# Two-layer hybrid block: the output projection's products reordered, and its first weights split within the scan

## The chip, the cores and the metric

The kernel runs on one core of one Trainium2 chip. A core has a matrix engine (TensorE, PE in the profile; PEld is its weight load), VectorE (DVE), ScalarE (ACT), GpSimd (POOL), a queue engine (SyncE, SP), an on-chip memory and a small accumulator memory (psum) that PE writes to. The metric is the device time of one execution in microseconds, lower is better.

## What is computed

Two layers of a block over 512 latent tokens and 256 context tokens, width 1024, in float32. The first layer's mixer is a bidirectional state-space scan beside a long convolution with a filter made by a small network; the second's is windowed attention. Both are followed by a gated feed-forward. The part that the change touches:

```python
def finish(y, z, hy):
    b, L = z.shape[:2]
    y = rmsnorm(y.reshape(b, L, SSD_WIDTH) * jax.nn.silu(z.astype(jnp.float32)), norm_g).astype(z.dtype)
    g = hyena_op(hy, hy_conv_w, hy_conv_b, hy_filt, hy_bias)
    return jnp.concatenate([y, g], axis=-1) @ w_out
...
        x = x + mod_l[2] * o_l
```

Here `y` is the scan's result, `g` the long convolution's ("Hyena"), and `w_out` the output projection, 2048 rows to 1024 columns.

## The kernel before

The activations lie feature by token: `X` (residual), `HN` (normed), eight tiles of 128 features by 768 tokens. Every product of this precision is made of three: a float32 value is split into a high part (a copy rounded to the fast format) and a low part (value minus high part), and PE adds high weight x high input, low weight x high input, and high weight x low input. A tile's three products run over 512 and 256 columns (`SEGS`).

Weights come in jobs (`JOBS`) of two halves, eight tiles of 128x128 each, into three slots in turn (`W[:, s]`). SyncE loads a half once the products that used its slot are counted in `blocks_done`. VectorE makes the high half (`split_high`, line 1623) into `WH`, of which there is one for both halves of a job; GpSimd makes the low half in the slot itself (`low`, line 2146, tile `weights_lo`). Each engine runs its own program in order and waits on counting semaphores; the order is written by hand.

The accumulators are three pairs of banks, `pair(0)` to `pair(2)`; a pair is free again when its reader has counted up `pair_free`.

The stages that matter, in order of time:
- The filter stage ends with twelve spectral products of the filter (`kd_mm`), each followed by a copy of one bank on ScalarE (line 1255) and two sums on VectorE (lines 1668 to 1672, counted in `kd_ev`). Meanwhile the first norm is applied: VectorE scales a tile of `X` into `HN` (`tile_first`, line 1616), ScalarE adds the shift (line 1215) and copies the high part (line 1217, `high_parts`), GpSimd makes the low part (line 2160). PE waits for all twelve `kd_ev` and starts the first input projection, `uv`, tile by tile (`both_by_tile`, lines 539 to 545).
- The scan: twelve steps, written as turns of two (`chunk_turns`). In a step PE makes the heads' products (943) in four groups, the score masks (904, 908), the spread decay (918), the carried product (928) and the states (951). ScalarE takes exponentials (1409, 1422); VectorE weighs the scores (`weigh`, 1873), multiplies the carried part (1880), adds it (1887) and adds the states (1894); GpSimd adds the carried part (`add_carried`, 2237), scales the input (2245) and the states (2253) and decays to the end (2262). Parts of two weight slots and the memory from 27648 on in `R` hold operands of the scan, and the last of these overlaps `WH`.
- The output projection, `out0` and `out0b`. Its first three jobs, G0 to G0+2, hold six half blocks: the Hyena parts of output tiles 0, 1 and 2, then the gated (scan) parts of the same three, so that PE can begin with Hyena inputs (`YGH[:, 1]`, `YGL[1]`, tile `hyena_lo`) while the scan's result is gated (VectorE, line 1926), squared and summed (ACT 1446, DVE 1932), normed through PE (`token_sums` 620, `token_spread` 626), scaled (DVE 1942) and split (ACT 1451, POOL 2291, tile `ssd_lo`). ScalarE's splits of both kinds are counted in `mix_hi`, GpSimd's in `mix_lo`. In the code before, G0 is cast when the scan is over, its two halves run tile by tile with highs and lows in turn, and the other four half blocks run one after another. VectorE adds each finished output tile to `X` (`residual`, 1959) and sums its squares (1599, 1600).

## Time and profile before

| | before |
|---|---|
| median of 3 runs | 2230.56 us (2226.12 to 2230.6) |
| the profiled execution's own time | 2231.3 us |
| its span | 2229.5 us |
| mean granted clock of PE | 0.967 of full |
| PE busy | 2111.7 us, 95% |
| weight load, DVE, ACT, POOL busy | 1682.1, 860.5, 441.2, 811.3 us |
| PE's share of the chain that ended last | 87% |

The span is the profiled part of one execution. Busy times are sums over the whole of it, and PE's are modelled, since its matmuls are pipelined. The granted clock has two levels, 1.2 GHz (0.50) and 2.4 GHz (1.00).

### The profile page before, as it was taken

To read this page: it belongs to the slowest core of one execution; us is meant where nothing else is said; L and a number is where in the kernel's file an instruction comes from. 1 tells how busy PE (TensorE), PEld (TensorE's weight loads), DVE (VectorE), ACT (ScalarE), POOL (GpSimd) and SP (SyncE) were. 2 spreads that over 40 slices of the span, in tenths; PEclk is the share of its full clock that TensorE was granted. 3 is DMA by queue.
4 is the path that set the end of the run, shared out by engine and by line. 5 is a ranking of instruction groups with operands and counts; after the bars stand their busy time and mean duration, and the time that the engine had idled before them with its cause. 6 is when DMAs were issued, how large, how long until landed. Compare 5 with 4: busy or idle time off the path is not lost.

```text
span 2229.5 us, 29888 instructions
## 1 busy us (share of the span) xinstructions
PE 2111.7 (95%) x11842; PEld 1682.1 (75%) x11842; DVE 860.5 (39%) x1245; ACT 441.2 (20%) x830; POOL 811.3 (36%) x438
## 2 busy tenths in 40 slices
PE   7989999999989978999999999998889999999997
PEld 2477668877877767878888888887666677888886
DVE  4633545203337664332121122233346663322334
ACT  3331110012335541031010010102026602100110
POOL 1443537122227755243223232224310134444443
PEclk9999989999989989999999999998989999999999
DMA  9444324342110011212112211121210022223222
GB/s 386 158 137 143 120 89 135 113 146 100 48 57 1 1 46 50 66 48 66 56 49 66 76 67 62 43 65 57 96 38 1 1 76 76 88 84 111 94 74 77
DMA packets 50791, 182.31 MB, mean 82 GB/s; under 512 B 5568, under 2 KB 6080, under 8 KB 49664
## 3 DMA queue, kind: packets, MB, share of 16 engines
q1 hardware_dynamic: 49600, 171.92, 22.8%
q10 hardware_dynamic: 576, 5.97, 0.7%
q0 software_dynamic: 512, 2.95, 0.4%
q8 instruction: 76, 1.25, 0.2%
q14 instruction: 27, 0.22, 0.0%
HBM read 178.72 MB, written 2.10 MB: 81 GB/s over the span
## 4 chain that ended last, share of the span: by engine, by line
PE 87%; DVE 5%; POOL 3%; ACT 2%; DMA 2%; issue 1%; DVEq 0%; ACTq 0%; SPq 0%
PE psum L516 21%; PE psum L521 21%; PE psum L517 21%; PE psum L1102 2%; PE psum L1090 2%; PE psum L1119 2%; PE psum L583 1%; PE psum L703 1%; DMA weights<-in_wall 1%; PE psum L739 1%; PE psum L918 1%; PE psum L539 1%; PE psum L545 1%; PE psum L943 1%; PE psum L540 1%
## 5 line engine op out<-in xcount | busy, mean ns | idle before, releaser
L2146 POOL TENSOR_TENSOR weights_lo<-weights,weights_hi 128x1024 fp32r<-128x1024 f32 (+1 forms) x228 | 504.9, 2215 | 989.4 <-DVE weights_hi L1623 989.4
L1623 DVE CAST weights_hi<-weights 128x1024 fp32r<-128x1024 f32 (+1 forms) x232 | 166.7, 720 | 887.1 <-PE psum L521 741.4
L521 PE MATMUL psum<-normed_lo,weights_hi 128*128 128x512 f32 x1760 | 506.9, 351 | 0.0
L516 PE MATMUL psum<-normed_hi,weights_hi 128*128 128x512 f32 x1088 | 391.6, 360 | 6.7 <-DVE weights_lo L1719 3.8
L517 PE MATMUL psum<-normed_hi,weights_lo 128*128 128x512 f32 x1088 | 373.9, 358 | 0.0
L521 PEld LDWEIGHTS psum<-normed_lo,weights_hi 128*128 128x128 f32 x1760 | 284.3, 189 | 16.5
L516 PEld LDWEIGHTS psum<-normed_hi,weights_hi 128*128 128x128 f32 x1088 | 204.8, 188 | 56.7 <-POOL weights_lo L2146 4.3
L516 PE MATMUL psum<-normed_first_hi,weights_hi 128*128 128x512 f32 (+1 forms) x672 | 232.2, 346 | 2.5 <-DVE weights_lo L1719 2.0
L517 PEld LDWEIGHTS psum<-normed_hi,weights_lo 128*128 128x128 f32 x1088 | 205.5, 189 | 34.8 <-issue 1.0
L517 PE MATMUL psum<-normed_first_hi,weights_lo 128*128 128x512 f32 (+1 forms) x672 | 212.7, 338 | 0.0
L516 PE MATMUL psum<-hidden_hi,weights_hi 128*128 128x512 f32 (+1 forms) x528 | 189.1, 358 | 0.0
L517 PE MATMUL psum<-hidden_hi,weights_lo 128*128 128x512 f32 (+1 forms) x528 | 178.9, 354 | 0.0
L521 PE MATMUL psum<-hidden_lo,weights_hi 128*128 128x512 f32 (+1 forms) x528 | 160.4, 358 | 0.0
L516 PEld LDWEIGHTS psum<-normed_first_hi,weights_hi 128*128 128x128 f32 x672 | 127.2, 189 | 38.2 <-issue 7.6
L517 PEld LDWEIGHTS psum<-normed_first_hi,weights_lo 128*128 128x128 f32 x672 | 127.2, 189 | 16.3 <-issue 1.2
L516 PEld LDWEIGHTS psum<-hidden_hi,weights_hi 128*128 128x128 f32 x528 | 99.1, 188 | 23.4
L517 PEld LDWEIGHTS psum<-hidden_hi,weights_lo 128*128 128x128 f32 x528 | 99.4, 188 | 15.1
L1731 DVE SCALAR_TENSOR_TENSOR temps<-psum,vectors,temps 128x511 f32<-128x511 f32 x112 | 63.8, 612 | 99.2 <-ACT temps L1277 98.3
L1468 ACT ACTIVATE temps<-psum 128x768 f32<-128x768 f32 (+1 forms) x44 | 31.1, 708 | 358.3 <-PE psum L521 353.8
L1472 ACT ACTIVATE hidden_hi<-temps 128x768 f32 (+3 forms) x44 | 32.6, 740 | 332.1 <-DVE temps L2013 332.1
L521 PEld LDWEIGHTS psum<-hidden_lo,weights_hi 128*128 128x128 f32 x528 | 87.1, 188 | 8.9
L516 PE MATMUL psum<-mixed_hi,weights_hi 128*128 128x512 f32 x224 | 77.8, 347 | 8.5 <-POOL weights_lo L2146 8.5
(312 smaller groups left out, 2973.1 us busy)
## 6 DMA issues: line engine op xcount, KB each, us to landing
weights<-in_wall SPq DMA_DIRECT2D x264, 512.0 KB, 3.9
weights<-in_wall SPq DMA_DIRECT2D x32, 384.0 KB, 3.2
weights<-in_wall SPq DMA_DIRECT2D x32, 320.0 KB, 3.0
residual<-in_xT SPq DMA_DIRECT2D x1, 3072.0 KB, 16.9
residual<-in_xT ACTq DMA_DIRECT2D x1, 3072.0 KB, 11.1
phase<-in_tab ACTq DMA_DIRECT2D x2, 1280.0 KB, 5.5
normed<-in_window SPq DMA_DIRECT2D x1, 1536.0 KB, 12.6
normed<-in_window POOLq DMA_DIRECT2D x1, 1536.0 KB, 9.5
```

The source lines that it names most:

```text
L516: mm(acc[:, lo:hi], WH[:, b, k, :], high[:, lo:hi], start=st, stop=False)
L517: mm(acc[:, lo:hi], WL[:, s, HALF * b + k, :], high[:, lo:hi], start=False, stop=False)
L521: ins = mm(acc[:, lo:hi], WH[:, b, k, :], low[:, lo:hi], start=False, stop=en)
L539: mm(accs[b][:, lo:hi], WH[:, b, k, :], high[:, lo:hi], start=k == 0, stop=False)
L1090: ins = mm(PSF[:, 1024 * e + at0:1024 * e + at1], QT[rows, 2 * g + j, b * P:b * P + P], KD[rows, g, key:key + at1 - at0], start=c in (0, 2 ...
L1102: ins = pe.transpose(PSF[:, 2048 + t * P:2048 + t * P + P], EX[:, n % 4, 1 + t * P:1 + t * P + P], C[:, IDENT, :])
L1119: ins = mm(PS[64 * e:64 * e + 64, 6, 0:256].rearrange("p (j c) -> p j c", j=2), VT[:, kt, 64 * g:64 * g + 64], heads_e, start=t == 0, stop ...
L1468: run(T[:, 0, lo:hi], pair(0)[:, lo:hi], ACT.Silu).then_inc(pair_free[0], 1)
L1472: run(at_row(HIDH, r)[:, lo:hi], T[:, 1, lo:hi], ACT.Copy).then_inc(hid_hi, 1)
L1623: dve.tensor_copy(WH[:, b, 0:n, :], W[:, s, HALF * b:HALF * b + n, :]).then_inc(w_hi, 1)
L1731: ins = STT(t[:, a:e], p[:, a + shift:e + shift], w, t[:, a:e], ALU.mult, ALU.add)
L2146: TT(WL[:, s, at, :], W[:, s, at, :], WH[:, b, 0:width(gs[0], b), :].bitcast(f32), ALU.subtract).then_inc(w_lo, 1)
```

## The change

At the end of the filter stage, ScalarE shifts only tile 0 between the last two bank copies (`shifted`) and splits it after the last one; VectorE scales tiles 0 and 1 as before but all others after the last pair of sums. At the projection, G0's halves are cast on VectorE and made low on GpSimd between the scan's first turns (`between`), into a home of their own, `WHX`, that lies where tiles 5 to 7 of `X` will be; G0+2 uses that home too, so that G0+1's is not waited for. PE runs all eight high products of G0's two halves first, then the lows, filling in the third half block's highs; the gated half blocks run all highs, then the lows of all three tile by tile. `X` is loaded in two parts, tiles 0 to 4 by ScalarE's queue as before and 5 to 7 by SyncE's after the six half blocks.

```diff
+        WHX = part("weights_first_hi", x_at, 4096, 2, HALF, P)
+        high_home = lambda g: WHX if g in (G0, G0 + 2) else WH
...
             body(0, (None, 4, 5, 5), False)
+            if between:
+                between(0)
             body(2, (5, 5, 4, 0), False)
+            if between:
+                between(1)
...
+                if at == G0 + 6:
+                    sp.wait_ge(blocks_done, 2 * G0 + 6)
+                    sp.dma_start(X[:, 5:KT, :], A["xT"][:, 5:KT, :]).then_inc(x2_in, 16)
...
-            both_by_tile([G0], 0, mixed, SEGS, mixed_waits, between_tiles, False)
...
+            def high_products(g, b, u, k, start):
+
+                s = g % SLOTS
+                high, _ = mixed(k)
+                for lo, hi in SEGS:
+                    mm(pair(u)[:, lo:hi], high_home(g)[:, b, k % KT, :], high[:, lo:hi], start=start, stop=False)
+                    mm(pair(u)[:, lo:hi], WL[:, s, HALF * b + k % KT, :], high[:, lo:hi], start=False, stop=False)
...
+            for b in range(2):
+                half_ready([G0], 0, b)
+                pair_ready([G0], 0, b)
+            for k in range(KT):
+                mixed_waits[0](k)
+                for b in range(2):
+                    high_products(G0, b, b, k, k == 0)
+            for k in range(KT):
+                mixed_waits[1](k)
+                for b in range(2):
+                    low_products(G0, b, b, k, False)
+                if k == 3:
+                    pe.wait_ge(yz_added, KT)
                     pe.wait_ge(yz_sums, 1)
                     token_sums(6).then_inc(yz_summed, 1)
-                if k == 7 and blocks == (0,):
+                    half_ready([G0 + 1], 0, 0)
+                    pair_ready([G0 + 1], 0, 0)
+                if k == 4:
                     pe.wait_ge(yz_rec, 1)
                     token_spread(6).then_inc(yz_spread, 1)
...
+                for h in ((), (), (), (0, 1), (2, 3), (4, 5), (6,), (7,))[k]:
+                    high_products(G0 + 1, 0, 2, h, h == 0)
+            for k in range(KT):
+                low_products(G0 + 1, 0, 2, k, False)
+
+            gated_parts = ((G0 + 1, 1, 0), (G0 + 2, 0, 1), (G0 + 2, 1, 2))
+            for g, b, u in gated_parts:
                 half_ready([g], 0, b)
-                tiles([g], pair(u), b, KT, gated, SEGS, False, True, gated_waits if u == 0 else None)
+                for k in range(KT):
+                    if u == 0:
+                        mixed_waits[0](KT + k)
+                    high_products(g, b, u, KT + k, False)
+            for k in range(KT):
+                mixed_waits[1](KT + k)
+                for g, b, u in gated_parts:
+                    low_products(g, b, u, KT + k, k == KT - 1)
...
-                    if n >= 10:
-                        high_parts(0, 0, 0, high=HNH0, ks=range(2) if n == 10 else range(2, KT))
+                    if n == 10:
+                        shifted(0, 0, 0, 0)
+            high_parts(0, 0, 0, high=HNH0, done=1)
...
-            act.dma_start(X[:, :, :], A["xT"]).then_inc(x_in, 16)
+            act.dma_start(X[:, 0:5, :], A["xT"][:, 0:5, :]).then_inc(x_in, 16)
...
-                        for k in (range(2), range(2, 4), range(4, KT))[n - 9]:
+                        for k in (range(2), (), range(2, KT))[n - 9]:
...
-            chunk_turns(dve, turn)
+            chunk_turns(dve, turn, between=lambda b: split_high([G0], 0, b))
...
-            for b in range(2):
-                split_high([G0], 0, b)
             for k in range(KT):
+                if k == 5:
+                    split_high([G0 + 1], 0, 0)
                 TT(XBC[:, k, :], XBC[:, k, :], Z[:, k, :], ALU.mult).then_inc(yz_ready, 1)
...
+                    dve.wait_ge(blocks_done, 2 * G0 + 3)
+                    split_high([G0 + 3], 0, 0)
                     for k in range(3):
+                        dve.wait_ge(blocks_done, 2 * G0 + 4 + k)
+                        if k == 0:
+                            split_high([G0 + 3], 0, 1)
                         residual(X[:, k, :], k, k)
...
-            chunk_turns(pool, turn)
-
-            low([G0], 0)
+            chunk_turns(pool, turn, between=lambda b: low([G0], 0, (b,)))
+            low([G0 + 1], 0, (0,))
```

The order on ScalarE at the end of the filter stage, from the eleventh bank copy on: `psum` to `phase` is the bank copy, `normed` with `mods` the shift, `normed_first_hi` the high part. Before:

```order
L1255 ACTIVATE phase<-psum 128x512 [waits kd_mm] x2
L1215 ACTIVATE normed<-normed,mods 128x512 [waits norm_mul]
L1215 ACTIVATE normed<-normed,mods 128x256
L1217 ACTIVATE normed_first_hi_53<-normed 128x768 [waits act_order]
L1215 ACTIVATE normed<-normed,mods 128x512 [waits norm_mul]
L1215 ACTIVATE normed<-normed,mods 128x256
L1217 ACTIVATE normed_first_hi_53<-normed 128x768 [waits act_order]
L1255 ACTIVATE phase<-psum 128x512 [waits kd_mm]
```

And with the change:

```order
L1304 ACTIVATE phase<-psum 128x512 [waits kd_mm] x2
L1258 ACTIVATE normed<-normed,mods 128x512 [waits norm_mul]
L1258 ACTIVATE normed<-normed,mods 128x256
L1304 ACTIVATE phase<-psum 128x512 [waits kd_mm,act_order]
L1266 ACTIVATE normed_first_hi_54<-normed 128x768
L1258 ACTIVATE normed<-normed,mods 128x512 [waits norm_mul]
```

The twelfth bank copy stands behind one shift instead of behind two whole tiles. On VectorE, the end of the scan and what follows (`phase<-phase` 128x768 is the gating multiply, `temps<-temps,psum` the sum of squares, the scaling reads `vectors` and `psum`). Before:

```order
L1887 TENSOR_TENSOR phase<-phase,psum 128x4x128 [waits step_y,step_zadd]
L1623 CAST weights_hi_49<-weights 128x1024 [waits w_loaded10,step_b,step_added]
L1623 CAST weights_hi_49<-weights 128x1024 [waits w_loaded11]
L1926 TENSOR_TENSOR phase<-phase 128x768 x8
L1934 COPY temps<-psum 128x768 [waits yz_square]
L1932 TENSOR_TENSOR temps<-temps,psum 128x768 [waits yz_added,yz_square] x7
L1937 MEMSET mark 128x1 [waits yz_added]
L1939 RECIPROCAL temps<-temps 128x12 [waits norm_sqrt]
L1942 SCALAR_TENSOR_TENSOR phase<-phase,vectors,psum 128x768 [waits yz_spread]
```

And with the change:

```order
L1937 TENSOR_TENSOR phase<-phase,psum 128x4x128 [waits step_y,step_zadd]
L1976 TENSOR_TENSOR phase<-phase 128x768 [waits step_b,step_added]
L1976 TENSOR_TENSOR phase<-phase 128x768 x4
L1673 CAST weights_hi_49<-weights 128x1024 [waits w_loaded20]
L1976 TENSOR_TENSOR phase<-phase 128x768 x3
L1984 COPY temps<-psum 128x768 [waits yz_square]
L1982 TENSOR_TENSOR temps<-temps,psum 128x768 [waits yz_added,yz_square] x7
L1987 MEMSET mark 128x1 [waits yz_added]
L1673 CAST weights_hi_49<-weights 128x1024 [waits w_loaded21]
```

The two casts of G0 are gone from here, and the first cast of G0+1 stands between the fifth and the sixth multiply. On GpSimd, one of the two places in the scan where a low part of G0 now stands, with the change (`phase<-phase,normed` adds the carried part, the three after it scale the input, the states and the decay to the end; before, the same rows stand without the second one):

```order
L2293 TENSOR_TENSOR phase<-phase,normed 128x4x128 [waits step_ze] x2
L2202 TENSOR_TENSOR weights_lo_50<-weights,weights_first_hi_51 128x1024 [waits weights_hi_ready]
L2301 TENSOR_TENSOR weights<-phase,temps 128x1024 [waits step_xde,step_y]
L2309 TENSOR_TENSOR temps<-temps 128x1024 [waits step_z]
L2318 TENSOR_TENSOR normed<-normed,temps 128x1024 [waits step_st,step_xdt]
```

What was done after the scan stands between the carried part and the next input's scaling.

## Rows read from the trace of the kernel before

**Rows 1.** PE's waits from 780 to 910 us: total, times, longest.
```profile
PE psum L516 <- POOL weights_lo L2146: 8.5, 1, 8.5
PE psum L539 <- POOL weights_lo L2146: 7.6, 1, 7.6
PE psum L545 <- POOL hyena_lo L2291: 4.9, 1, 4.9
```

**Rows 2.** Timeline of PE: start, duration, line, tiles, count [idle before].
```profile
800.52 0.66 PE L943 MATMUL psum<-normed,weights 128*64 128x128 f32 x8 [1.17 <-DVE normed L1873]
...
821.27 0.40 PE L539 MATMUL psum<-mixed_hi,weights_hi 128*128 128x512 f32 x1
...
822.67 0.86 PE L545 MATMUL psum<-hyena_lo,weights_hi 128*128 128x512 f32 x4
823.36 0.39 PE L539 MATMUL psum<-mixed_hi,weights_hi 128*128 128x512 f32 x1
...
829.69 1.39 PE L620 MATMUL psum<-consts,temps 128*128 128x2 f32 x12
...
833.13 1.50 PE L626 MATMUL psum<-consts,temps 128*128 128x128 f32 x12
```

**Rows 3.** Timeline of DVE in the projection's first part.
```profile
802.02 1.29 DVE L1623 CAST weights_hi<-weights 128x1024 fp32r<-128x1024 f32 x2
803.23 11.32 DVE L1926 TENSOR_TENSOR phase<-phase 128x768 f32<-128x768 f32 x8
...
815.53 7.30 DVE L1932 TENSOR_TENSOR temps<-temps,psum 128x768 f32<-128x768 f32 x7
...
834.67 2.86 DVE L1942 SCALAR_TENSOR_TENSOR phase<-phase,vectors,psum 128x768 f32<-128x768 f32 x3 [3.02 <-PE psum L626]
...
882.07 0.69 DVE L1623 CAST weights_hi<-weights 128x1024 fp32r<-128x1024 f32 x1 [3.44 <-PE psum L521]
882.68 1.14 DVE L1959 SCALAR_TENSOR_TENSOR residual<-psum,mods,residual 128x512 f32<-128x512 f32 x2
```

**Rows 4.** Timeline of ACT there: the Hyena high parts.
```profile
799.62 5.98 ACT L1439 ACTIVATE mixed_hi<-phase 128x768 fp32r<-128x768 f32 x8
```

**Rows 5.** Timeline of POOL there.
```profile
802.79 5.74 POOL L2146 TENSOR_TENSOR weights_lo<-weights,weights_hi 128x1024 fp32r<-128x1024 f32 x2 [3.11 <-DVE weights_hi L1623]
814.63 14.41 POOL L2291 TENSOR_TENSOR hyena_lo<-phase,mixed_hi 128x768 fp32r<-128x768 f32 x8 [6.11 <-DVE phase L1926]
```

**Rows 6.** Windows of 4 us: busy time of each engine, granted clock, DMA share, GB/s.
```profile
core 0: us, PE busy (x) PEld busy (x) DVE busy (x) ACT busy (x) POOL busy (x), PEclk, DMA share, GB/s
...
804.00:808.00 4.00, 0.00 (x0) 0.00 (x0) 4.00 (x2) 3.78 (x6) 4.00 (x2) 0.50 1.00 399
...
136.00:140.00 4.00, 1.95 (x15) 1.05 (x8) 3.32 (x6) 0.00 (x0) 0.00 (x0) 1.00 0.76 247
```

**Rows 7.** Timeline of PE at the end of the filter stage.
```profile
105.45 5.32 PE L703 MATMUL psum<-phase 128*128 128x512 f32 x12
115.30 0.80 PE L539 MATMUL psum<-normed_first_hi,weights_hi 128*128 128x512 f32 x1 [4.54 <-DVE phase L1672]
...
119.31 0.63 PE L539 MATMUL psum<-normed_first_hi,weights_hi 128*128 128x512 f32 x1
```

**Rows 8.** Timeline of ACT there.
```profile
109.58 1.11 ACT L1215 ACTIVATE normed<-normed,mods 128x512 f32<-128x512 f32 x2
...
113.35 0.58 ACT L1255 ACTIVATE phase<-psum 128x512 f32<-128x512 f32 x1
```

**Rows 9.** Timeline of DVE there.
```profile
113.96 0.69 DVE L1668 TENSOR_TENSOR phase<-phase,psum 128x512 f32<-128x512 f32 x1 [0.87 <-ACT phase L1255]
```

**Rows 10.** Timeline of DVE in the third step of the scan: the weighing.
```profile
681.05 0.69 DVE L1873 TENSOR_TENSOR normed<-normed 128x512 f32<-128x512 f32 x1
...
683.30 1.98 DVE L1873 TENSOR_TENSOR normed<-normed 128x512 f32<-128x512 f32 x1
```

**Rows 11.** Timeline of POOL and ACT at that step's end.
```profile
689.31 1.71 POOL L2237 TENSOR_TENSOR phase<-phase,normed 128x512 f32<-128x512 f32 x1
...
691.12 1.02 ACT L1409 ACTIVATE normed<-psum 128x1024 f32<-128x1024 f32 x1 [1.99 <-PE psum L918]
```

More of the change, by code:

```diff
@@ L339, in build_kernel @@
         a_ch, v_ch, g_ch = sem("act_order"), sem("dve_order"), sem("pool_order")
-        x_in, c_in, v_in, small_in, t3_in, t4_in, win_in, rope_in = (
-            sem(n) for n in ("x_in", "c_in", "v_in", "small_in", "t3_in", "t4_in", "win_in", "rope_in"))
+        x_in, x2_in, c_in, v_in, small_in, t3_in, t4_in, win_in, rope_in = (
+            sem(n) for n in ("x_in", "x2_in", "c_in", "v_in", "small_in", "t3_in", "t4_in", "win_in", "rope_in"))
         silu_c, mods_a, mods_b = sem("silu_c_ready"), sem("mods_a_ready"), sem("mods_b_ready")
@@ L411, in job_turns, with chunk_turns @@
                 body([first + r], 0, r)
-        def chunk_turns(eng, body, unrolled=False):
+        def chunk_turns(eng, body, unrolled=False, between=None):
             body(0, (None, 4, 5, 5), False)
+            if between:
+                between(0)
             body(2, (5, 5, 4, 0), False)
+            if between:
+                between(1)
             middle = lambda i: body(i * 2 + 4, (i * -1 + 4, i * 1, i * -1 + 3, i + 1), False)
@@ L993, in _ @@
             mixed_waits = waits(mix_hi, 0, mix_lo, 0)
-            def between_tiles(k, blocks):
-                if k == 5 and blocks == (0, 1):
+            def high_products(g, b, u, k, start):
[4 more added lines that the diff above has]
+                    mm(pair(u)[:, lo:hi], WL[:, s, HALF * b + k % KT, :], high[:, lo:hi], start=False, stop=False)
@@ new lines, in low_products @@
+            def low_products(g, b, u, k, stop):
+                _, low = mixed(k)
+                for lo, hi in SEGS:
+                    ins = mm(pair(u)[:, lo:hi], high_home(g)[:, b, k % KT, :], low[:, lo:hi], start=False, stop=stop)
+                if k % KT == KT - 1:
+                    ins.then_inc(blocks_done, 1)
+            for b in range(2):
[5 more added lines that the diff above has]
+                    high_products(G0, b, b, k, k == 0)
@@ L1000, in between_tiles @@
                     pe.wait_ge(yz_rec, 1)
                     token_spread(6).then_inc(yz_spread, 1)
-            both_by_tile([G0], 0, mixed, SEGS, mixed_waits, between_tiles, False)
-            gated = lambda k: mixed(KT + k)
-            gated_waits = [lambda k, wait=wait: wait(KT + k) for wait in mixed_waits]
-            half_ready([G0 + 1], 0, 0)
-            pe.wait_ge(yz_added, KT)
-            tiles([G0 + 1], pair(pair_ready([G0 + 1], 0, 0)), 0, KT, mixed, SEGS, True, False)
-            for g, b, u in ((G0 + 1, 1, 0), (G0 + 2, 0, 1), (G0 + 2, 1, 2)):
-                half_ready([g], 0, b)
-                tiles([g], pair(u), b, KT, gated, SEGS, False, True, gated_waits if u == 0 else None)
+                for h in ((), (), (), (0, 1), (2, 3), (4, 5), (6,), (7,))[k]:
+                    high_products(G0 + 1, 0, 2, h, h == 0)
@@ L1208, in root, with shifted, high_parts @@
                 run(RS[0][:, 0:n], NS[:, 0:n], ACT.Sqrt, scale=1.0 / D, bias=vec("eps", 0)).then_inc(n_sqrt, 1)
-            def high_parts(muls, layer, shift, segs=SEGS, high=HNH, ks=range(KT)):
-                lo, hi = segs[0][0], segs[-1][1]
-                for k in ks:
-                    act.wait_ge(n_mul, muls + k + 1)
-                    for j, (a, b) in enumerate(segs):
-                        ins = run(HN[:, k, a:b], HN[:, k, a:b], Id, bias=MOD[:, layer, 8 * shift + k, j:j + 1])
-                    ch.link(ins)
+            def shifted(muls, layer, shift, k, segs=SEGS):
+                act.wait_ge(n_mul, muls + k + 1)
+                for j, (a, b) in enumerate(segs):
+                    ins = run(HN[:, k, a:b], HN[:, k, a:b], Id, bias=MOD[:, layer, 8 * shift + k, j:j + 1])
+                ch.link(ins)
+            def high_parts(muls, layer, shift, segs=SEGS, high=HNH, done=0):
+                lo, hi = segs[0][0], segs[-1][1]
+                for k in range(KT):
+                    if k >= done:
+                        shifted(muls, layer, shift, k, segs)
                     run(high[:, k, lo:hi], HN[:, k, lo:hi], ACT.Copy).then_inc(hn_hi, 1)
@@ L1984, in body @@
                         x = at_row(X, k)
+                        if name == "out0" and isinstance(r, int) and r == 2:
+                            dve.wait_ge(x2_in, 16)
                         if gs[-1] + 1 == len(JOBS):
@@ L2291, in _ @@
                 TT(YGL[j][:, k, :], src, YGH[:, j, k, :].bitcast(f32), ALU.subtract).then_inc(mix_lo, 1)
-                if n in (KT + 2, KT + 4):
-                    low([G0 + 1], 0, (n // 2 - 5,))
-            for g in (G0 + 1, G0 + 2):
-                low([g + 1], 0)
+                if n == KT - 1:
+                    low([G0 + 1], 0, (1,))
+                if n in (KT + 1, KT + 3):
+                    low([G0 + 2], 0, ((n - KT) // 2,))
+            low([G0 + 3], 0)
             next_low("out0b", 5)
```

17 lines of the change are left out of this document (8 added, 9 removed).

## The prediction, made before the changed kernel ran

> **What bounds the kernel now.** I looked first at where the matrix engine (PE) waits, since it is busy nearly all of the span and the chain that ended last is mostly its own; then at what each wait is released by; then at the other engines in those windows.
>
> At the start of the output projection PE stands still three times: 7.6 us for GpSimd's low part of the first weights, 4.9 us for the first low part of the Hyena tile, 8.5 us for the low part of the second weights [rows 1]. That is 21.0 us. The scan's last product starts at 800.52 and ends at 801.2 [rows 2]; the weights were cast only then (802.02) and their low parts made from 802.79 to 808.53 [rows 3, 5].
>
> What PE could do at once was ready: ScalarE had the eight high parts of the Hyena half done by 805.6 [rows 4]. The stage ends at 882.0, when the cast at 882.07 is released by the last of six half blocks [rows 3].
>
> Idle PE also loses its clock. 804 to 808 shows no matmul and a granted clock of 0.50; the pause inside 136 to 140 (busy 1.95 of 4 us) left it at 1.00 [rows 6]. After the idle 4.54 us before 115.30 a tile of two blocks took 119.31 - 115.30 = 4.01 us, of which warm 823.36 - 821.27 = 2.09 [rows 2, 7].
>
> At the end of the filter stage PE has finished the last spectral product at 110.77 and starts the first weights' products at 115.30: VectorE's last pair ran at 113.96, since ScalarE's copy of that bank came at 113.35, behind two tiles of high parts that it had begun at 109.58 [rows 7 to 9].
>
> **The change, on the times of before.**
>
> *Filter end.* ScalarE now shifts one tile (1.11 us from 109.58, to 110.7) and then waits for PE, so its bank copy (0.58) runs at about 110.9 to 111.5. VectorE's pair then starts at 111.6 in place of 113.96: 2.4 us earlier [rows 8, 9]. PE starts at 112.9 after 2.1 us idle. The pause inside 136 to 140 was 2.0 us and cost no clock [rows 6], so I take the clock as kept: the first 5.3 us of matmuls (115.30 to about 120.6, at half clock) then shrink by 2.6 us. The tiles' high and low parts come 1.9 us apart, less than the 2.09 us of a warm tile, so they don't bind. Together 5.0 us, or 2.4 if the clock falls all the same. ScalarE's table load follows later by under 1 us and now overlaps the next weights' load; for that I take off 0.5. Gain 4.5 (2.0 to 5.0).
>
> *Scan.* Two casts of the first projection weights, and their two low parts on GpSimd, now sit after the second and the fourth step of the scan. A cast costs 0.65 us (1.29 for two) and a low part 2.87 (5.74 for two) [rows 3, 5]. Neither is free there: VectorE's weighing of the score tile took 0.69 us when it started ahead of GpSimd's work and 1.98 beside it [rows 10]. GpSimd ends its add of the carried part at 691.02, and ScalarE's exponential starts at 691.12 [rows 11]: no slack worth the name, so 2.87 us on GpSimd moves that exponential later, and behind it VectorE's decay product and the heads' products on PE. How much of it PE has in hand no row says; the waits of a step are spread over four engines, so I take about half, 1.5 us for an insertion and 3.0 for two. Bounds: one cast hidden wholly, 0.3 together; or each low part paid in full with a cast, (2.87 + 0.65) x 2 = 7.0.
>
> The Trainium skill (GPSIMD Engine Reference, section 1, Specifications) says that GpSimd shares its SBUF interfaces with VectorE and contends with VectorE instructions that have two SBUF inputs or run in a two-port mode. The trace agrees (0.69 against 1.98 us). By that rule alone the insertions cost on both engines at once, so it speaks against this part of the change; by VectorE's 0.65 us alone the scan would lose 1.3 us.
>
> *Projection, first part.* PE goes on at 801.2 with the high products of both halves of the first weights for eight tiles: 1.40 us a tile (822.67 - 821.27), 11.2 us, to 812.4, warm, none waiting [rows 2, 4]. Meanwhile VectorE starts its eight gating multiplies at 802.0 instead of 803.23. Of before's eight (11.32 us) the two beside GpSimd's low parts took about 6 and six took 5.25, 0.88 each [rows 3]. Now five run alone (to 806.4), then a cast (807.1), one more, one that waits for GpSimd's low part of the second weights (ends about 810), one more: 811.8, against 814.55. GpSimd then makes the Hyena low parts, 1.80 us each (14.41 for eight) [rows 5]: the first is ready at 813.7, the fourth at 819.1. PE's low products of a tile take 0.69 us, so it idles 1.3 us and then 1.1 us three times, 4.6 in all, and has the fourth done at 819.8. VectorE's sum of squares (copy and seven adds, 8.4 us [rows 3]) is done at 820.3, so the token sums start at 820.4: another 0.6 us idle.
>
> *From 820.4* PE has all it needs in order: token sums 1.3, two tiles of the third half block 1.4, low tile 0.7, spread 1.3 to 1.5 [rows 2], then six tiles of that half block (4.2) and three low tiles (2.1), its own lows 2.8, three gated half blocks' highs 16.8, their lows 8.4: 39 us, to 859.4. Is anything late? The scaling by the norm can start at 825.2 (before: 834.67), 0.95 us a tile [rows 3], with two casts and a wait of about 1.2 us for the first half block's end; the last high part comes at about 839, and PE reaches it at 839. GpSimd has, from the eighth Hyena low part (826), three weight low parts (8.6) and eight gated ones (14.4, as the Hyena ones): done by 849, while PE wants the first gated low tile at 851. Neither holds PE.
>
> *A new wait at the end.* The last three half blocks now all finish within 0.7 us. The next weights use the first of these accumulators, which VectorE frees only after a cast (0.69) and the residual (1.14) [rows 3]: PE starts about 1.3 us late, at 860.7. Queued behind are two more residuals with squares on VectorE (some 13 us in all); the next cast is due when PE is 16.8 us further, so that is covered. The residual's last three tiles load later on SP's queue, needed some 50 us later: nothing. The third to fifth weight loads are released later too, and the casts of two of them are 10 us off or more: nothing.
>
> So the stage ends at 860.7 instead of 882.0: 21.3. The clock is the open term: PE works 0.7 of 1.8 us from 813.7 to 820. No row shows whether that keeps the clock; if not, the 4 to 5 us from 820.4 run at half speed and cost 2.5 us. I take half, 1.3. Gain 20.0 (17.5 to 22).
>
> **Sum.** 4.5 - 3.0 + 20.0 = 21.5 us. Against the profiled execution's own 2231.3 us that is 2209.8; it stood 0.7 above the median of the runs, so I predict **2209** us. After the projection PE never idles for long, so nothing takes the gain back.
>
> **Rivals.**
> - *The clock falls at both places* (filter end and the sparse low products). For it: the idle at the filter end is 2.1 us, at the edge of what the trace shows as harmless, and 812 to 820 would be 35% busy. Price 2.6 + 1.3 more: 2213. Chance 0.18.
> - *The scan pays*: GpSimd becomes its pace for two or three steps and VectorE weighs beside it. Price 4 us more, up to all bounds: 2213 to 2218. Chance 0.15. This is where the skill's rule would take it if contention were paid in full.
> - *The scan hides it* and the clock stays: 2209 - 3.0 - 1.3 = 2205 or a little less. Chance 0.10.
> - *The change does not do what it says*: the gated part stays bound by VectorE and GpSimd. If the scaling began at 834.67 as before, GpSimd's eight gated parts and two weight low parts (20.1 us, from about 836) would end at 856, and PE at 860 to 862; so the worst here is a few us, unless the cast between the multiplies stalls. Result 2218 to 2226. Chance 0.04.
> - *Slower than before*: the cast after the fifth multiply waits for a load that is issued only when the scan ends. VectorE is in order, so every multiply, sum and scaling behind it would be late with it. Before, that load was on its way with 399 GB/s in 804 to 808 [rows 6], four halves of 0.5 MB, so the first should be there by 805, ahead of 806.4. It turns the result only from 22 us of delay. Chance 0.02, with 0.02 more for a result near before.
> - My forecast, 2206 to 2212: 0.49.
>
> **How the numbers follow.** The range 2204 to 2217 takes in the forecast, the clock rival, the hidden scan and most of the costly scan: about 0.85, less what I may have missed. This kernel's measurement can't tell under 0.2% (4.5 us) from no change. Faster by more: 0.95; within: 0.03; slower: 0.02.
>
> **What would show it.** Right: no wait of PE for weights' low parts after the scan; waits of 1 to 1.5 us, four or five, for Hyena low parts; PE's first products of the uv weights 2.4 us after the last spectral product instead of 4.5, at clock 1.00; the two steps of the scan with the casts longer by 1 to 2 us each; a pause near 1.3 us ahead of the fourth projection weights. Wrong: a wait above 2 us in the gated highs; GpSimd's low part ahead of the exponential in more than two steps; PE at 0.50 from 816 to 826.

## The result, and the profile after

| | before | after |
|---|---|---|
| time, median (range) | 2229.3 us (2225.4 to 2230.6), 5 runs | 2216.1 us (2209.9 to 2218.3), 5 runs |
| profiled execution: time, span | 2231.3, 2229.5 us | 2218.3, 2216.5 us |
| mean granted clock of PE | 0.967 | 0.971 |

The ratio is 0.9936 (95% interval 0.9921 to 0.9950): 14.3 us faster, 11.1 to 17.6. Forecast were 2209 us, range 2204 to 2217. Direction and range held, the range by 0.9 us; the gain was put 7 us too high.

PE's waits from 780 to 910 us, which answer to [rows 1] (columns: total, times, longest, in us):

```profile
PE psum L1016 <- POOL hyena_lo L2346: 2.0, 2, 1.2
PE psum L952 <- DVE normed L1923: 1.4, 2, 1.2
PE psum L525 <- DVE residual L2012: 1.1, 1, 1.1
PE psum L905 <- ACT weights L1444: 0.2, 1, 0.2
```

The three long waits (21.0 us) are gone. What is left are two short ones for Hyena low parts and the new one at the end of the stage. PE's timeline there, which answers to [rows 2]:

```profile
803.13 0.66 PE L952 MATMUL psum<-normed,weights 128*64 128x128 f32 x8 [1.16 <-DVE normed L1923]
803.72 0.50 PE L1009 MATMUL psum<-mixed_hi,weights_first_hi 128*128 128x512 f32 x1
...
816.38 0.96 PE L1016 MATMUL psum<-hyena_lo,weights_first_hi 128*128 128x512 f32 x4 [1.16 <-POOL hyena_lo L2346]
818.17 5.21 PE L1016 MATMUL psum<-hyena_lo,weights_first_hi 128*128 128x512 f32 x12 [0.82 <-POOL hyena_lo L2346]
823.17 2.55 PE L629 MATMUL psum<-consts,temps 128*128 128x2 f32 x12
825.59 0.77 PE L1009 MATMUL psum<-mixed_hi,weights_hi 128*128 128x512 f32 x1
...
829.58 2.43 PE L635 MATMUL psum<-consts,temps 128*128 128x128 f32 x12
...
867.47 0.50 PE L525 MATMUL psum<-mixed_hi,weights_hi 128*128 128x512 f32 x1 [1.14 <-DVE residual L2012]
```

PE goes on 0.6 us after the scan's last product began, and the high products run warm. The token sums begin at 823.17, 20.0 us behind that product; forecast were 820.4 - 800.5 = 19.9. So far the working was right. From there it was not: the token sums take 2.55 us, the spread begins at 829.58. The windows say why (columns as in [rows 6]):

```profile
815.00:817.00 2.00, 0.84 (x5) 0.59 (x5) 1.79 (x3) 1.51 (x3) 2.00 (x2) 1.00 0.00 0
817.00:819.00 2.00, 1.18 (x5) 0.77 (x5) 1.79 (x3) 1.52 (x3) 2.00 (x2) 0.71 0.00 0
819.00:829.00 10.00, 9.73 (x34) 7.95 (x34) 3.31 (x5) 0.60 (x2) 10.00 (x6) 0.50 0.01 2
829.00:831.00 2.00, 2.00 (x10) 1.90 (x10) 0.00 (x0) 0.00 (x0) 2.00 (x2) 0.50 0.00 0
831.00:833.00 2.00, 2.00 (x13) 1.84 (x12) 0.96 (x2) 0.00 (x0) 0.52 (x1) 0.87 0.00 0
```

In the pauses between the low products (PE busy 0.84 and 1.18 of 2 us) the granted clock falls from 1.00 to 0.50, and it stays there while PE is busy again, 9.73 of 10 us. It comes back only past 831.

To follow the gain through the program I use three stretches that can be read in every trace. *Filter*: from the start of the last spectral block (PE's group of 12, 5.32 us long) to the cast near 151 us. *Scan*: from its first group of two weighings to its last weighing. *Stage*: from the start of the scan's last product to the cast behind the eighth half block of the projection, the second after the stage. The marks, of the kernel before (lines 1873 and 1623) and after (lines 1923 and 1673):

```profile
655.53 2.36 DVE L1873 TENSOR_TENSOR normed<-normed 128x512 f32<-128x512 f32 x2
...
799.77 0.69 DVE L1873 TENSOR_TENSOR normed<-normed 128x512 f32<-128x512 f32 x1 [0.63 <-ACT normed L1422]
...
898.87 0.69 DVE L1623 CAST weights_hi<-weights 128x1024 fp32r<-128x1024 f32 x1 [7.68 <-PE psum L521]
```

```profile
653.26 2.36 DVE L1923 TENSOR_TENSOR normed<-normed 128x512 f32<-128x512 f32 x2
...
802.38 0.69 DVE L1923 TENSOR_TENSOR normed<-normed 128x512 f32<-128x512 f32 x1 [0.62 <-ACT normed L1472]
...
884.62 0.69 DVE L1673 CAST weights_hi<-weights 128x1024 fp32r<-128x1024 f32 x1 [6.96 <-PE psum L530]
```

Scan: 144.2 us before, 149.1 after: 4.9 longer. Stage: 898.87 - 800.52 = 98.4 before, 884.62 - 803.13 = 81.5 after: 16.9 shorter. Filter: 46.1 before, 43.4 after: 2.7 shorter. That makes 14.7, beside the 14.3 of the timed runs. The unchanged stretches of the two profiled executions differ by 1 to 3 us either way (the last spectral block itself starts at 105.45 before and at 107.90 after). In all fourteen traces of this document the unchanged way from the cast near 151 us to the scan's first weighings took between 500.3 and 504.3 us. So a single trace can price these three stretches, and not the whole kernel.

The filter's end, which answers to [rows 7]: PE's group of 12, then its first uv products, and the next pause.

```profile
107.90 5.32 PE L712 MATMUL psum<-phase 128*128 128x512 f32 x12
115.29 0.50 PE L548 MATMUL psum<-normed_first_hi,weights_hi 128*128 128x512 f32 x1 [2.07 <-DVE phase L1722]
...
137.09 0.50 PE L525 MATMUL psum<-normed_first_hi,weights_hi 128*128 128x512 f32 x1 [2.66 <-DVE weights_lo L1769]
```

```profile
138.00:140.00 2.00, 2.00 (x10) 1.71 (x9) 1.82 (x4) 0.00 (x0) 0.60 (x1) 0.65 1.01 303
140.00:142.00 2.00, 2.00 (x8) 1.71 (x7) 0.00 (x0) 0.00 (x0) 2.00 (x2) 0.50 0.92 309
142.00:144.00 2.00, 2.00 (x13) 1.74 (x13) 0.00 (x0) 0.00 (x0) 1.89 (x1) 1.00 0.36 147
```

The first part came as forecast: 7.39 us from the group of 12 to the uv products in place of 9.85, and these start at the short, warm duration. But the pause behind the uv block, 2.05 us before, is now 2.66, and here the clock falls.

### The profile page after: what moved, and what is told of

Its sections match the earlier page's. It is cut to its first block, busy times and chain, and to the rows that moved or that the text cites. A ratio compares the mean times of both kernels' runs of the same rounds, so it can differ in the third digit from the quotient of the medians.

```text
span 2216.5 us, 29871 instructions
## 1 busy us (share of the span) xinstructions
PE 2114.8 (95%) x11842; PEld 1681.7 (76%) x11842; DVE 856.6 (39%) x1245; ACT 440.6 (20%) x830; POOL 815.9 (37%) x438
## 3 DMA queue, kind: packets, MB, share of 16 engines
q1 hardware_dynamic: 49744, 173.10, 22.9%
## 4 chain that ended last, share of the span: by engine, by line
PE 87%; DVE 5%; POOL 3%; DMA 2%; issue 2%; ACT 1%; SPq 0%; ACTq 0%; DVEq 0%; POOLq 0%
PE psum L525 21%; PE psum L530 21%; PE psum L526 21%; PE psum L1146 2%; PE psum L1134 2%; DMA weights<-in_wall 2%; PE psum L1163 2%; PE psum L712 1%; PE psum L748 1%; PE psum L592 1%; POOL weights_lo L2202 1%; PE psum L675 1%; PE psum L927 1%; PE psum L952 1%; DVE normed L1923 1%
## 5 line engine op out<-in xcount | busy, mean ns | idle before, releaser
L2202 POOL TENSOR_TENSOR weights_lo<-weights,weights_hi 128x1024 fp32r<-128x1024 f32 (+1 forms) x224 | 497.3, 2220 | 986.3 <-DVE weights_hi L1673 986.3
L2071 DVE TENSOR_TENSOR hidden_lo<-temps,hidden_hi 128x768 f32 (+3 forms) x44 | 60.7, 1379 | 44.0 <-ACT hidden_hi L1522 44.0
## 6 DMA issues: line engine op xcount, KB each, us to landing
normed<-in_window POOLq DMA_DIRECT2D x1, 1536.0 KB, 10.2
```

Source lines behind the costliest of these rows:

```text
L2071: TT(at_row(HIDL, r)[:, lo:hi], T[:, 1, lo:hi], at_row(HIDH, r)[:, lo:hi].bitcast(f32), ALU.subtract).then_inc(hid_ready, 1)
L2202: TT(WL[:, s, at, :], W[:, s, at, :], high_home(gs[0])[:, b, 0:width(gs[0], b), :].bitcast(f32), ALU.subtract).then_inc(w_lo, 1)
```

## Experiments

All kernels at a glance; the stretches are in us, read from each one's trace; the ratio is to the kernel before, run beside it on the same chip. Its medians there were 2228.3 to 2230.2 us, so medians of different rows can be off by some 2 us against each other.

| kernel | median us | ratio (95%) | filter | scan | stage |
|---|---|---|---|---|---|
| before | 2229.3 | 1 | 46.1 | 144.2 | 98.4 |
| changed | 2216.1 | 0.9936 (0.9921-0.9950) | 43.4 | 149.1 | 81.5 |
| filter_alone | 2228.5 | 1.0004 (0.9995-1.0013) | 43.7 | 144.2 | 98.3 |
| without_filter | 2217.5 | 0.9952 (0.9937-0.9968) | 46.3 | 149.0 | 78.5 |
| scan_in_gap | 2209.1 | 0.9910 (0.9897-0.9922) | 43.5 | 145.2 | 80.4 |
| table_early | 2216.0 | 0.9947 (0.9934-0.9960) | 42.0 | 148.5 | 80.2 |
| filled_gaps | 2211.0 | 0.9919 (0.9905-0.9933) | 42.1 | 149.1 | 77.3 |
| split_after_scan | 2213.2 | 0.9924 (0.9911-0.9937) | 42.7 | 144.2 | 84.6 |
| residual_first | 2213.4 | 0.9927 (0.9909-0.9945) | 42.5 | 150.3 | 80.6 |
| gap_fill_residual | 2207.0 | 0.9898 (0.9885-0.9911) | 43.3 | 145.4 | 76.6 |
| pauses_filled | 2203.8 | 0.9880 (0.9863-0.9897) | 41.7 | 145.1 | 76.7 |
| three_without_filter | 2208.8 | 0.9911 (0.9896-0.9926) | 44.6 | 145.7 | 76.7 |
| three_again | 2207.9 | 0.9895 (0.9877-0.9914) | 43.3 | 145.1 | 76.7 |
| old_end_filled | 2209.3 | 0.9901 (0.9881-0.9920) | 43.4 | 145.1 | 76.6 |

**The filter edit alone, and all but it.** The first kernel is the one before with the edits of `high_parts`, of ScalarE's copies and of VectorE's tiles (the whole of the diff there); the second is the changed kernel without them.

> The kernel before with the edit at the filter end alone. Two readings of the trace after. Mine: the products of the uv weights start 2.5 us earlier and stay at clock 1.00, but they then end before the load of the next weights, which shares the DMA engines with the table load, so the pause behind them grows from 2.05 to about 2.7 us, the clock falls to 0.50 for some 3.5 us and takes back 1.7 us: 2.5 us faster in all, ratio about 0.9989. Rival, the prediction's term: the 4.5 us are kept, and the loss in the profiled run was chance: ratio 0.998.

> The changed kernel with the filter stage's end put back as before; scan and projection as changed. If the parts add up, it is 14.3 - 2.5 = 12 us faster than before (ratio 0.9946); by the prediction's 4.5 us for the filter end it would be 14.3 - 4.5 = 10 us faster (0.9956).

Alone the edit is worth 0.9 us of loss, between 1.1 us of gain and 2.9 of loss: neither reading fits, though its trace shows the stretch 2.4 us shorter and PE's two waits about as expected (2.1 and 3.0 us, the second expected at 2.7, with the clock at 0.50 behind it). Without the edit the changed kernel is 10.7 us faster than before (7.1 to 14.0), which does not tell 10 from 12. More on this below.

Its trace gave something else. The stage took 78.5 us here against 81.5, with not one instruction of it changed. The sparse low products are the same; the clock fell 7 us later, after the token sums had begun, and was back after 3.4 us in place of 13.7.

**The two insertions, moved by one operation each.**

```diff
@@ VectorE, turn of the scan
                     weigh(s, d, 3)
+                    if d == 1 and isinstance(s0, int) and s0 < 4:
+                        split_high([G0], 0, s0 // 2)
                     if not (last and d == 1):
                         decay_carried(s + 1, 0)
-            chunk_turns(dve, turn, between=lambda b: split_high([G0], 0, b))
+            chunk_turns(dve, turn)
@@ GpSimd, turn of the scan
                     add_carried(s, t, 1)
+                    if d == 1 and isinstance(s0, int) and s0 < 4:
+                        low([G0], 0, (s0 // 2,))
                     if not (last and d == 1):
                         add_carried(s + 1, chunks[d + 2], 0)
-            chunk_turns(pool, turn, between=lambda b: low([G0], 0, (b,)))
+            chunk_turns(pool, turn)
```

> The changed kernel with each of the two casts and low parts in the scan moved by one operation: the cast ahead of the decay product for the next step, the low part ahead of the add of the carried part. There VectorE stands idle 2.95 us and GpSimd 2.71 us in every step, waiting for PE. Theory, the place decides: a low part (2.87) fits the 2.71 us, so an insertion costs about 0.2 us and the scan's 4.9 us of extra time shrink to 0.5 or less: 4 to 4.5 us faster than the changed kernel, ratio to before about 0.9917. Rival, the contention decides: GpSimd's 2.9 us slow VectorE's two-input products wherever they stand, and the scan stays 3 to 5 us longer: ratio 0.993 to 0.994, as the changed kernel.

GpSimd in the step of the first insertion: the changed kernel, then this one.

```profile
675.26 1.71 POOL L2293 TENSOR_TENSOR phase<-phase,normed 128x512 f32<-128x512 f32 x1
679.30 1.65 POOL L2293 TENSOR_TENSOR phase<-phase,normed 128x512 f32<-128x512 f32 x1 [2.34 <-DVE normed L1930]
680.91 2.81 POOL L2202 TENSOR_TENSOR weights_lo<-weights,weights_first_hi 128x1024 fp32r<-128x1024 f32 x1
683.68 2.34 POOL L2301 TENSOR_TENSOR weights<-phase,temps 128x1024 f32<-128x1024 f32 x1
```

```profile
675.18 1.71 POOL L2295 TENSOR_TENSOR phase<-phase,normed 128x512 f32<-128x512 f32 x1
677.53 2.37 POOL L2204 TENSOR_TENSOR weights_lo<-weights,weights_first_hi 128x1024 fp32r<-128x1024 f32 x1 [0.63 <-DVE weights_first_hi L1673]
679.86 1.72 POOL L2295 TENSOR_TENSOR phase<-phase,normed 128x512 f32<-128x512 f32 x1
681.55 1.89 POOL L2303 TENSOR_TENSOR weights<-phase,temps 128x1024 f32<-128x1024 f32 x1
```

In the changed kernel GpSimd waits 2.34 us for VectorE's decay product, adds the carried part, makes the low part, and only then scales x, which it could have begun at 680.9. Moved ahead of the add, the low part fills that wait, and the scaling begins at 681.55, 2.4 us sooner counted from each scan's first weighing (653.26 and 653.56). The scan falls from 149.1 to 145.2 us, 1.0 over the kernel before (with the insertions in their old place it is 148.5 to 150.3 in five traces), and the kernel to 2209.1 us (ratio 0.9910 against 0.9936). The place decided. VectorE's weighings still meet GpSimd's work (2.43 us for the one at 681.57), so contention is there but was not what the 4.9 us were made of.

**ScalarE's table load, 13 us earlier.** The two lines that wait for the last spectral product and start the load stand ahead of `high_parts(0, 0, 0, high=HNH0, done=1)` instead of behind it and the helpers.

> The changed kernel with ScalarE's table load (1.3 MB) issued ahead of its high parts, some 13 us earlier, so that it has landed when the x0 weights' next load is issued. Theory: the cast of those weights no longer waits for DMA, the pause of PE falls from 2.66 to about 2.0 us, and the clock stays at 1.00 behind it: 0.6 + 1.7 = 2.3 us faster than the changed kernel. Rival: the load alone takes as long (the wait is for its issue), or the pause of 2 us costs the clock as well: no change.

The time did not change (2216.0). The trace refutes the theory on the load: with the table long landed the first of the next weights' loads still took 4.5 us to land, and the pause was 2.8 us.

```profile
132.65 0.69 DVE L1673 CAST weights_hi<-weights 128x1024 fp32r<-128x1024 f32 x1 [1.39 <-DMA weights<-in_wall]
```

This load is issued 3.8 us ahead of PE's pause, before (133.00, 136.77) as after (130.66, 134.43). It took 3.4 to 4.0 us in the five traces with a slow start of the uv block (before, without_filter, residual_first, split_after_scan, three_without_filter), and 4.3 to 4.7 in the seven others without fillers in the pauses (the changed kernel, filter_alone, scan_in_gap, this one, filled_gaps, gap_fill_residual, three_again). What slows it is open. In this trace the clock stayed at 1.00 behind 2.8 us, and the filter stretch was 42.0.

**Gaps of the low products filled.** This adds to the result the product of the two low parts of three tiles, a term that the reference's arithmetic holds and both kernels leave out as too small.

```diff
@@ PE, low_products
                     ins = mm(pair(u)[:, lo:hi], high_home(g)[:, b, k % KT, :], low[:, lo:hi], start=False, stop=stop)
+                if g == G0 and k < 3:
+                    for lo, hi in SEGS:
+                        mm(pair(u)[:, lo:hi], WL[:, g % SLOTS, HALF * b + k, :], low[:, lo:hi], start=False, stop=False)
```

> The changed kernel, with a second product (weights' low part times Hyena's low part, 0.7 us a tile for the two half blocks) behind each of the first three low products, where PE otherwise waits 1.1 us for GpSimd. No product starts later by it. Clock theory: in four traces of this stage the granted clock fell to 0.50 here and stayed there for 3, 9, 10 and 13 us, and the stage took 78.5, 80.2, 80.4 and 81.5 us from the scan's last product to the end of the eighth half block. With 1.4 of each 1.8 us busy the clock stays at 1.00 and the stage takes 77.5 to 78.5: 2 to 4 us faster than the changed kernel's 2216 us. Rival: the stage is bound by VectorE and GpSimd behind the sums; the clock stays up and the stage still takes 80 us or more, no gain.

The windows of its stage (the scan's last product starts at 797.66), and the token sums and the spread in PE's timeline:

```profile
809.00:812.00 3.00, 1.85 (x11) 1.42 (x10) 2.69 (x3) 2.27 (x4) 3.00 (x3) 1.00 0.00 0
812.00:815.00 3.00, 2.71 (x15) 1.91 (x14) 2.79 (x3) 1.63 (x2) 3.00 (x3) 1.00 0.01 3
815.00:825.00 10.00, 9.85 (x66) 8.71 (x65) 4.87 (x8) 1.97 (x3) 10.00 (x6) 1.00 0.01 2
825.00:835.00 10.00, 10.00 (x59) 8.78 (x58) 8.57 (x7) 4.19 (x5) 10.00 (x6) 1.00 0.48 157
```

```profile
817.14 1.40 PE L629 MATMUL psum<-consts,temps 128*128 128x2 f32 x12
...
820.60 1.50 PE L635 MATMUL psum<-consts,temps 128*128 128x128 f32 x12
```

The clock stays at 1.00. The token sums take 1.40 us in place of 2.55, the spread comes 22.9 us behind the scan's last product in place of 26.5, and the stage takes 77.3 us: 4.2 shorter than the changed kernel's, with 2.1 us more of products in it (three times 0.70). The other three traces with these products unfilled and the residual in its place (without_filter, table_early, scan_in_gap) had 78.5 to 80.4, so the filling is worth 1.2 to 4.2 us. The median is 2211.0 us, 5 less than the changed kernel's, though the two intervals overlap. VectorE and GpSimd had time in hand behind the sums, so the rival falls.

**The split back behind the scan, with the new order of the projection.**

```diff
@@ VectorE
-            chunk_turns(dve, turn, between=lambda b: split_high([G0], 0, b))
+            chunk_turns(dve, turn)
...
             dve.wait_ge(s_bst, STEPS)
+            for b in range(2):
+                split_high([G0], 0, b)
             for k in range(KT):
@@ GpSimd
-            chunk_turns(pool, turn, between=lambda b: low([G0], 0, (b,)))
+            chunk_turns(pool, turn)
+            low([G0], 0)
```

> The changed kernel with the first weights' casts and low parts back behind the scan; the new order of the projection is kept. By the traces: the scan gives back 4.9 us (weighing from first to last 144.2 in place of 149.1). PE then waits 7.6 us after the scan as before and starts cold, so its high products end 22 us behind the scan's last product and the sums start at about 24.6; with the insertions the sums start at 20.0 but the half clock up to 28.6 costs 4.3. So the stage takes the same 81 to 82 us, and the kernel is 4 to 5 us faster than the changed one, about 2211.5. Rival, the prediction's account: the split in the scan costs 3.0 and saves the 7.6 us wait (less 0.6): this kernel is 4 us slower than the changed one, 2220.

```profile
797.59 0.66 PE L952 MATMUL psum<-normed,weights 128*64 128x128 f32 x8 [1.16 <-DVE normed L1923]
805.82 0.77 PE L1009 MATMUL psum<-mixed_hi,weights_first_hi 128*128 128x512 f32 x1 [7.58 <-POOL weights_lo L2204]
```

The wait of 7.6 us is back in full, the scan takes 144.2 us, and the stage 84.6: 3.1 us more than the changed kernel's and not the 7 that the wait alone suggests. That difference has the clock in it: behind the start of the token sums it was down for 3.4 us here, and for 13.7 around them in the changed kernel. Beside without_filter, where it was down for 3.4 us too, the stage is 6.1 us longer. The median is 2213.2 us, 2.9 less than the changed kernel's, with intervals that overlap. So where the change put it, the split within the scan paid 4.9 us and got 3 to 6 back, no gain that the times show. In the idle places it pays 1.0. As far as the times can tell, the gain of the change is the new order of the products (this kernel also holds the filter edit).

**Residual ahead of the cast at the stage's end.** `residual(X[:, k, :], k, k)` stands ahead of `split_high([G0 + 3], 0, 1)`.

> The changed kernel with the order of two VectorE instructions turned at the end of the stage: residual of the first accumulator ahead of the cast of the fourth weights' second half. Theory: PE's wait ahead of those weights (1.1 us for cast and residual) falls to about 0.6, since only the residual stands ahead; the cast is due 8 us later. 0.6 us faster, less than the times can tell, so the row decides. Rival: none of weight; if the wait stays at 1.1, the semaphore it waits for is another.

```profile
PE psum L525 <- DVE residual L2012: 0.5, 1, 0.5
```

The wait falls from 1.1 to 0.5 us, as the theory has it.

**The three edits together, twice, without the filter edit, and with fillers in the pauses.** The fillers are products that nothing reads, into a bank that is free there. `old_end_filled` has the filter stage's end as before, with five of them in the first, longer pause.

```diff
@@ PE
             assert not early
+            for _ in range(2):
+                mm(PS[:, 4, :], C[:, IDENT, :], C[:, 0:4, :].rearrange("p a b -> p (a b)"), start=True, stop=True)
             pe.wait_ge(kd_ev, 12)
...
             uv(0, [AT["uv"]], by_tile=waits(hn_hi, 0, hn_ready, 0))
+            for _ in range(6):
+                mm(PS[:, 4, :], HNH0[:, 0, 0:P], HNH0[:, 0, 0:512], start=True, stop=True)
```

> Three edits on the changed kernel together: casts and low parts of the scan in the idle places ahead of the carried part's add, the three gaps of the low products filled, residual ahead of the cast. If they add up: scan 4 us (ratio 0.991 measured for it alone, 2209 us), clock kept another 2 to 3 us, residual 0.6: 2205 to 2207 us. If the clock theory is wrong: 2208 to 2209.

> The kernel of three edits together once more, on this chip, as the measure for the two others: 2205 to 2208 us, ratio near 0.990.

> The kernel of three edits together with the filter stage's end as it was before. The filter edit alone measured as no change (ratio 1.0004, 0.9995 to 1.0013), while every trace with it reaches the cast at about 151 us 2.4 to 4.1 us sooner, counted from the last spectral block. If the traces are right, this kernel is 2.5 to 4 us slower than the one of three edits in the same call; if the timed runs of the edit alone are, it is within 1 us of it.

> The kernel of three edits together, with products that nobody reads put into PE's two pauses around the first uv block: two of 128 x 512 in f32 ahead of it (a pause of 2.07 us), six of 128 x 512 behind it (2.1 to 3.0 us), all into a bank that is free there. Clock theory for the filter end: in ten traces the granted clock fell to 0.50 behind one of the two pauses in six of the eight with the new order there; with the pauses half filled it stays at 1.00 at both places, and the time from the last spectral block's start to the cast at about 151 us is 42.0 us, as in the two traces without a fall, in place of 42.5 to 43.7: 0.5 to 1.7 us faster than the same kernel without the fillers. Rival: the fillers delay what follows, or the falls cost nothing that the next wait would not have cost: no gain.

> The three edits together with the filter stage's end as before, and the products that nobody reads in both pauses: five of 128 x 512 in f32 (4.1 of the 4.5 us) ahead of the first uv block, six behind it. It tells apart what the filter edit is worth in VectorE's earlier pair and what in the clock. If the clock stays at 1.00 at both places, the way from the last spectral block's start to the cast at about 151 us takes 2.3 us less than the 46.1 us of before, 43.8, against 41.7 measured with the new order and the fillers; the kernel then stands 2 us above the 2203.8 us of that one, near 2206, ratio 0.989. If the filter edit's whole worth is the clock, the two are equal.

The three edits add up: 2207.0 and 2207.9 us, and the clock stays at 1.00 through the stage in all five kernels that hold them. With the fillers it holds at both pauses too, and the kernel takes 2203.8 us, 4 less than three_again, which ran beside it, more than the 0.5 to 1.7 expected, though the intervals overlap; the filter stretch is 41.7 us against 43.3. Its windows over the uv block and the pause behind it:

```profile
116.00:134.00 18.00, 18.00 (x111) 14.49 (x109) 7.80 (x15) 13.66 (x21) 13.55 (x8) 1.00 0.29 105
134.00:138.00 4.00, 2.99 (x15) 1.93 (x12) 2.94 (x4) 0.00 (x0) 0.00 (x0) 1.00 0.90 286
138.00:142.00 4.00, 4.00 (x25) 3.47 (x24) 1.77 (x4) 0.00 (x0) 2.65 (x2) 1.00 0.97 334
```

On the filter edit the times and the traces give different sizes. With the clock held in both orders the traces give it 43.4 - 41.7 = 1.7 us, and the ratios 4.7 us (0.9901 against 0.9880), with intervals that overlap. With the clock left to itself the traces give 1.3 (44.6 against 43.3) to 2.7, and the times 0.9 (2208.8 against 2207.9) or, for the edit alone, nothing, with an interval that ends at 1.1 us of gain. The fillers are no clearer: with the old end the stretch is 1.2 us shorter with them (43.4 against 44.6), but the kernel took 2209.3 us, where 2206 was expected, and 2208.8 without them. Each of these four ratios is known to 3 to 4 us. A worth of 1 to 2 us for the edit, and as much for the fillers, is nearest to all of it; the times don't show either.

## Why the prediction was right, and where its terms were off

The number held with some luck: all three terms were off the same way, by 3.1, 1.9 and 1.8 us, and another microsecond would have left the range.

*Projection, 20.0 us forecast, 16.9 in the trace.* Each step up to the token sums came within 0.2 us, with two errors that cancelled. VectorE's multiplies were through at 812.3, 9.1 us behind the scan's last product, where I had 811.8 - 800.5 = 11.3, for I let them wait for GpSimd; it was GpSimd that waited. Its low part of the second weights took 4.80 us, not 2.87:

```profile
809.58 2.69 DVE L1976 TENSOR_TENSOR phase<-phase 128x768 f32<-128x768 f32 x3
```

```profile
809.74 4.80 POOL L2202 TENSOR_TENSOR weights_lo<-weights,weights_hi 128x1024 fp32r<-128x1024 f32 x1 [7.45 <-DVE weights_hi L1673]
814.50 14.72 POOL L2346 TENSOR_TENSOR hyena_lo<-phase,mixed_hi 128x768 fp32r<-128x768 f32 x8
```

It ended 2.3 us after VectorE's third multiply, so nearly all of it came behind them. The Trainium skill (SBUF — State Buffer, SBUF: two separate sides) says that of a VectorE operation with two SBUF inputs and one of GpSimd, whichever starts first has the shared ports for its whole length and the other is blocked. The trace agrees: VectorE started 0.16 us sooner. That GpSimd stayed out over three multiplies in a row, that sentence does not say; it is read from the 4.80 us.

The term that failed is the loss of clock, priced at 2.5 us and taken by half, 1.3. The clock did fall, and in the changed kernel's trace it cost more than the whole 2.5: filled_gaps, which keeps it, takes 4.2 us less for the stage. I had let it recover in 4 to 5 us; by the windows above it stood at 0.50 for 13.7 us, and what the prediction named as a sign of being wrong, "PE at 0.50 from 816 to 826", came true. The other traces of the same order (without_filter, table_early, scan_in_gap) lost 1.2 to 3.1 us by it, and by them the projection gained 18.0 to 19.9 us, so the profiled execution had the dearest fall of the four. With the clock kept, the stage is 98.4 - 77.3 = 21.1 us shorter than before, 21.7 with the residual first (76.7). Forecast without a clock loss were 21.3. So the order of products was costed rightly and only the clock was mis-sized.

*Scan, 3.0 forecast, 4.9 measured* (scan_in_gap and split_after_scan agree with the traces). The size was inside its bounds, but the sentence "no slack worth the name" was wrong. It was read at the add on which the step depends, and is right for the place between two steps. GpSimd's wait of 2.3 to 2.7 us a step lies one operation earlier, and the prediction never asked where in its order the low part comes.

*Filter end, 4.5 forecast, 2.7 in the traces.* VectorE's earlier pair was right (2.46 us). The clock was kept at the first pause, as taken, in seven of the nine traces without fillers there. What failed is the next pause, for which only 0.5 us was taken off, for the table load: the pause behind the uv block grew by 0.6 us, and the clock fell behind it, which the prediction had at nothing. Where it stayed up at both pauses (table_early, filled_gaps) the stretch took 42.0 and 42.1 us, 4.0 less than before and near the forecast; in the five traces where it fell behind the uv block, 43.3 to 43.7. So the fall took back 1.2 to 1.7 of the 2.6 us of the warm start. table_early shows that the table load was not the cause.

*Rivals.* "The clock falls at both places" (2213, 0.18) is nearest to what happened, though in the filter stage it was another pause than the one named. "The scan pays" came half true. "The scan hides it" and "does not do what it says" were wrong; the cast after the fifth multiply waited for nothing. The wait at the stage's end was forecast at 1.3 us and is 1.14.

*Left open*: why the timed runs of the filter edit alone show no gain, and what makes the load behind the uv block slower after a fast start of that block (4.3 to 4.7 us against 3.4 to 4.0).

## What to carry to other kernels

Where work is inserted into a tight loop of several engines, look in each engine's own order for the operation that waits longest and put the work right ahead of it; one place further on cost 2 us a time here. Where a reordering leaves the matrix engine with short pauses instead of one long one, price a fall of its clock too, and if the pauses can't be closed, products that cost nothing there keep it up (by the traces 1.2 to 4.2 us in the projection, and 1.6 at the filter's end). Price each part of a change alone: the part that looked needed (the split within the scan) brought nothing that the times show where it stood.

## What the runs showed of the hardware

The clock's fall and return are not a fixed price. Read from windows of 1 us, the granted clock stood at 0.50 in the projection for 3.4 us (without_filter), 10.2 us (scan_in_gap, table_early, residual_first) and 13.7 us (the changed kernel), with the same products on PE there, and in the longest PE was busy for 9.73 of 10 us from 819 to 829. With the gaps filled it stayed at 1.00 in six traces of six. Behind the uv block the clock fell in five of seven traces with a pause of 2.6 to 3.0 us and in none of the five with 1.7 to 2.3; ahead of it, behind 2.07 us, in two of nine. The Trainium skill (TensorE: Matmul & The Clock Gate, Part 1) says that the number of slow matmuls at a kernel's start differs between runs of the same kernel. The traces show as much for falls in the middle of one. It may also be what spreads the times: without_filter ran in 2212.0 to 2224.1 us, while the kernel before stayed within 6 us beside it; that link was not tested.
